# A two-block transformer forward pass on one core: the first weight tile in halves behind four products of zeros, the last three tiles of the last gate by halves of the tokens

## The reference

```python
def first_block(x, p, norm_mix_g, w_in, ...):
    h = rmsnorm(x, norm_mix_g[i])
    u = h @ w_in[i]                       # start of the program
    ...

def second_block(x, p, ln1, w_in, ..., ln3, w_pp, w_pg, rel_bias, ln_f):
    ...
        h3 = rmsnorm_2(x, ln3[i])
        x = x + jax.nn.sigmoid(h3 @ w_pg[i]) * (p[i] @ w_pp[i])   # the last gate
    return rmsnorm_2(x, ln_f)

def rmsnorm_2(x, g):
    xf = x.astype(jnp.float32)
    y = xf * lax.rsqrt(jnp.mean(xf * xf, axis=-1, keepdims=True) + EPS)
    return (y * g.astype(jnp.float32)).astype(x.dtype)
```

## Time and profile before

| | |
|---|---|
| median of 3 runs | 2126.29 us (2119.96 to 2127.86) |
| profiled execution | 2122.81 us, of which the span of the trace is 2120.9 us |
| mean granted TensorE clock | 0.981 of full speed |
| busy share: TensorE, VectorE, ScalarE, GpSimd | 96%, 47%, 37%, 14% |
| first real product of TensorE | 9.12 us after the span's start |
| last product of the last gate | starts at 2095.73 us |

### The profile page before, as it was taken

How to read it: one execution, slowest core, us unless ns; L and a number is a source line. 1 busy time by engine, 2 the same in 40 slices (tenths; PEclk the granted TensorE clock), 3 DMA queues, 4 the chain that set the end, 5 groups by cost and what they waited for, 6 DMA issues and landing times.

```text
span 2120.9 us, 27569 instructions
## 1 busy us (share of the span) xinstructions
PE 2039.4 (96%) x11518; PEld 1625.5 (77%) x11518; DVE 994.1 (47%) x1534; ACT 783.3 (37%) x1233; POOL 293.1 (14%) x292
## 2 busy tenths in 40 slices
PE   7999999999999999999899999998999999999996
PEld 5767677777888778888676788886788888888884
DVE  5665555444643233346845444446643442333354
ACT  5573222113444323235523233335332343322344
POOL 2001221210221001012200000001310220100124
PEclk9999999899999999999999999999999999999998
DMA  4121111112623332223321122221222233222221
GB/s 174 60 70 60 46 52 41 46 42 76 209 87 109 112 102 90 99 100 119 120 67 56 57 70 80 82 88 60 82 97 100 100 120 109 100 90 99 100 80 50
DMA packets 59843, 185.46 MB, mean 87 GB/s; under 512 B 6551, under 2 KB 11799, under 8 KB 59592
## 3 DMA queue, kind: packets, MB, share of 16 engines
q1 hardware_dynamic: 59720, 183.71, 25.5%
HBM read 173.46 MB, written 10.22 MB: 87 GB/s over the span
## 4 chain that ended last, share of the span: by engine, by line
PE 85%; DVE 5%; ACT 4%; issue 3%; POOL 1%; DMA 1%; SPq 0%; DVEq 0%; POOLq 0%; ACTq 0%
PE P L545 24%; PE P L547 23%; PE P L546 23%; DVE AREN L1649 1%; PE P L820 1%; PE P L856 1%; PE P L910 1%; PE P L849 1%; DVE WLO L1656 1%; POOL AREN L2318 1%; PE P L908 1%; PE P L805 1%; ACT WHI L1104 1%; POOL AREN L2321 1%; DVE AREN L1652 1%
## 5 line engine op out<-in xcount | busy, mean ns | idle before, releaser
L545 PE MATMUL P<-HH,WHI 128*128 128x512 f32 x1528 | 628.7, 411 | 22.1 <-DVE WLO L1656 11.8
L547 PE MATMUL P<-HH,WLO 128*128 128x512 f32 x1528 | 602.4, 394 | 0.0
L546 PE MATMUL P<-HL,WHI 128*128 128x512 f32 x1528 | 601.5, 394 | 0.0
L1656 DVE TENSOR_TENSOR WLO<-RAW,WHI 128x1024 fp32r<-128x1024 f32 x303 | 382.3, 1262 | 180.4 <-ACT WHI L1104 178.6
L1104 ACT ACTIVATE WHI<-RAW 128x1024 fp32r<-128x1024 f32 x303 | 318.8, 1053 | 377.3 <-PE P L547 374.3
L545 PEld LDWEIGHTS P<-HH,WHI 128*128 128x128 f32 x1528 | 290.2, 190 | 102.8 <-issue 20.2
L545 PE MATMUL P<-ARR,WHI 128*128 128x512 f32 (+1 forms) x904 | 352.1, 390 | 6.5 <-DVE WLO L1656 2.9
L547 PE MATMUL P<-ARR,WLO 128*128 128x512 f32 (+1 forms) x904 | 350.7, 388 | 0.0
L546 PE MATMUL P<-ARR,WHI 128*128 128x512 f32 (+1 forms) x904 | 350.7, 388 | 0.0
L547 PEld LDWEIGHTS P<-HH,WLO 128*128 128x128 f32 x1528 | 290.3, 190 | 63.6
L546 PEld LDWEIGHTS P<-HL,WHI 128*128 128x128 f32 x1528 | 290.9, 190 | 54.7 <-issue 1.2
(11 more groups left out here) (297 smaller groups left out, 1559.3 us busy)
## 6 DMA issues: line engine op xcount, KB each, us to landing
RAW<-in_w_in_dram SPq DMA_DIRECT2D x118, 512.0 KB, 3.3
RAW<-in_w_ff_dram SPq DMA_DIRECT2D x64, 512.0 KB, 3.3
RAW<-in_w_ml_dram SPq DMA_DIRECT2D x64, 512.0 KB, 3.2
RAW<-in_w_out_dram SPq DMA_DIRECT2D x16, 512.0 KB, 3.4
RAW<-in_w_pg_dram SPq DMA_DIRECT2D x16, 512.0 KB, 3.2
AREN<-in_xT_dram SPq DMA_DIRECT2D x16, 256.0 KB, 6.4
s_gates<-AREN SPq DMA_DIRECT2D x16, 256.0 KB, 2.0
RAW<-in_w_ab_dram SPq DMA_DIRECT2D x8, 512.0 KB, 3.5
```

The costliest lines, as they stand in the source:

```text
L545: e.matmul(out, hi, H[0][:, s], start=first, stop=False)
L546: e.matmul(out, hi, H[1][:, s], start=False, stop=False)
L547: return e.matmul(out, lo, H[0][:, s], start=False, stop=last)
L1656: e.tensor_tensor(WLO[n % NSPL][:, :], RAW[n % NRAW][:, :], WHI[n % NSPL][:, :].bitcast(F32), ALU.subtract).then_inc(*D.dve.sig("wlo", n))
```

## The change

At the start, SyncE loads the first half of tile 0 (slices 0 to 3) ahead of everything, then `x0`, `vec`, `x1`, tile 1, `x2`, `x3`, the second half of tile 0, `x4` to `x7` and tile 2. ScalarE and VectorE split the halves separately. TensorE first multiplies a block of zeros, which GpSimd writes, four times into an unused bank. The second tile runs three rows behind the first instead of two. The sum of squares of the first norm is formed by two engines: GpSimd adds squares 0 to 3, VectorE squares 4 to 7 and the two halves. The squares have eight buffers of their own, and `WHI` of tile 2 stands between squares 3 and 4. The work on `lam` moves behind the first finished tile, and the first norm's total goes to bank 2 instead of 7.

At the end, tiles 5, 6 and 7 of the last gate are multiplied for tokens 0 to 255 first and then for tokens 256 to 511, in six half tiles. The multiplication by the embedding moves from GpSimd to VectorE for these, the last square too. The total of half 0 stands in TensorE's program behind the first half tile of half 1. The outputs are multiplied in five wide operations (one of them, four blocks, on GpSimd), with five stores.

```diff
+def last_rows():
+    yield from lead2(5, 0)
+    for u in range(6):
+        for k in range(8):
+            yield 5 + u, k
+
+def last_steps(j, k):
+    at = {(0, 7): "evac", (1, 0): "sigmoid", (1, 1): "mult", (1, 2): "add", (1, 3): "square", (1, 4): "sum"}
+    return [(5 + u % 3, u // 3, at[j - 5 - u, k]) for u in range(6) if (j - 5 - u, k) in at]
...
-                g = units(("attn",), T_AT, lead2(12, 2), H1, hx("HX"), ev("attn"), (0, 1, 6, 7))
-                for j, k in lead2(12, 2):
+                w.wait_ge(K.pool.at("zero"))
+                for _ in range(4):
+                    e.matmul(bank(3), ar(52)[:, 0:128], ar(52), start=True, stop=True)
+                g = units(("attn",), T_AT, lead2(12, 3), H1, hx("HX"), ev("attn"), (0, 1, 6, 7))
+                for j, k in lead2(12, 3):
                     if (j, k) == (3, 0):
-                        total("n1")
+                        total("n1", 2)
...
+                for half, banks in ((0, (4, 5, 6)), (1, (1, 2, 3))):
                     cs = slice(256 * half, 256 * half + 256)
...
+                    for t, b in zip((5, 6, 7), banks):
+                        w.wait_ge(D.dve.at("wlo", T_PG2 + t), free.get(b))
+                        for k in range(8):
+                            d = row(bank(b)[:, 0:256], T_PG2 + t, k, (H3[k][0][:, cs], H3[k][1][:, cs]), k == 0, k == 7)
+                            if k == 7:
+                                d.then_inc(*D.pe.sig("pg2", t, half))
+                                if half and t == 5:
+                                    last_total(0, 7)
+                            yield
+                last_total(1, 0)
+
+            def last_total(half, b):
...
+                w.wait_ge(N.pool.at("add", "n8", 6, half), K.pool.at("one"), free.get(b))
+                e.matmul(bank(b)[:, 0:256], cst("ones"), ar(acc)[:, cs], start=True, stop=False)
+                w.wait_ge(N.dve.at("sq", "n8", 7, half))
+                e.matmul(bank(b)[:, 0:256], cst("ones"), ar(tmps[1])[:, cs], start=False,
+                         stop=True).then_inc(*N.pe.sig("sum", "n8", half))
...
+            def result(half, i, n):
+                cs = slice(256 * half, 256 * half + 256)
+                y = v3(ar(8, 8), 8)[:, i:n, cs]
+                w.wait_ge(N.act.at("rs", "n8", half), D.act.at("xg", n - 1, half) if n > 5 else D.act.at("xg", n - 1))
+                mul(y, y, ar(6)[:, cs].unsqueeze(1).to_broadcast([128, n - i, 256])).then_inc(*D.dve.sig("y", half, n))
...
+                    if (j, k) == (9, 1):
+                        y = v3(ar(8, 8), 8)[:, 0:4, 0:256]
+                        w.wait_ge(N.act.at("rs", "n8", 0), *[D.act.at("xg", i) for i in range(4)])
+                        mul(y, y, ar(6)[:, 0:256].unsqueeze(1).to_broadcast([128, 4, 256])).then_inc(*D.pool.sig("y"))
...
             def begin():
+                name, i = TILES[0]
+                load("first", 0, RAW[0][:, 0:512], A[name][i, :, 0:512])
                 for j in range(8):
                     load(f"x{j}", 0, ar(j), A["xT"][:, T * j:T * (j + 1)])
                     if j == 0:
                         load("vec", 0, VEC[:, :], A["vecs"])
-                    if j in (0, 3, 7):
-                        weights((0, 3, 7).index(j))
+                    if j == 1:
+                        weights(1)
+                    if j == 3:
+                        load("raw0", 0, RAW[0][:, 512:1024], A[name][i, :, 512:1024])
+                weights(2)
```

More of the change, by code:

```diff
@@ L1264, in dense @@
                 yield from mlp("m", T_ML2, "n6", "H3b", "ln3", "n7")
-                for j, k in [*lead2(7, 0), *[(7, k) for k in range(16)]]:
-                    if j < 7:
+                for j, k in last_rows():
+                    if j < 6:
                         ahead(T_PG2, j, k, True)
@@ L1303, in whi_mg2, with last_rs @@
+            def last_rs(half, b):
+                rs = ar(6)[:, 256 * half:256 * half + 256]
+                w.wait_ge(N.pe.at("sum", "n8", half))
+                e.activation(rs, bank(b)[:, 0:256], ACT.Ln, scale=1.0 / 1024, bias=EPS6).then_inc(
+                    *N.act.sig("ln", "n8", half))
+                w.wait_ge(N.act.at("ln", "n8", half))
+                e.activation(rs, rs, ACT.Exp, scale=-0.5).then_inc(*N.act.sig("rs", "n8", half))
             def whi_mg2(i, k):
@@ L2330, in begin @@
             def begin():
+                e.memset(ar(52), 0.0).then_inc(*K.pool.sig("zero"))
                 for i, (a, v) in enumerate(((EPS6, 1e-6), (EPS5, 1e-5), (EPSG, 64e-5))):
```

215 lines of the change are left out of this document (124 added, 91 removed).

## The result

| | before | after |
|---|---|---|
| median, us (runs) | 2125.97 (8) | 2110.36 (8) |
| lowest to highest | 2119.96 to 2127.86 | 2103.59 to 2119.75 |
| ratio, 95% interval | | 0.9945, 0.9927 to 0.9963 |
| profiled execution, us | 2122.81 | 2113.17 |
| its span, us; mean granted clock | 2120.9; 0.981 | 2111.4; 0.984 |

By the ratio the change made the kernel faster by 0.55% (0.37 to 0.73), which is just past what I had called the limit of no change. (The ratios in this document are the recorded ones and need not be the quotient of the medians, here 0.9927, or of the means, here 0.9936.) The forecast was 2116.5 with a range from 2109 to 2123. The profiled executions differ by 9.6 us, the medians by 15.6. The last sections come back to that difference.

The account below looks back on a forecast made before the run. TensorE, busy in 96% of the span, was taken as the bound, leaving its waits, slow stretches and tail to save. Start 3.0 plus end 5.0 gave 8.0 us: 2114.8 or 2118.3 by baseline, middle 2116.5, range 2109 to 2123.

Parts of the forecast that it names:

- one fall behind it at 1.4: Start: TensorE's clock falls once at the wait before the third row, costing 1.7 us less 0.3 hidden, so 1.4.
- Both old waits: Start: TensorE's waits of 2.22 us for tile 2's `WLO` and 0.87 us for the first norm's root go, gaining 3.1.
- The first term, 1.3: Start: as an unbroken run at 2.4 GHz it begins at 10.6 instead of 11.87, gaining 1.3 us (0.2 to 2.3).
- Steps of 0.43 us after 14 us: Start: listed sign of a wrong prediction, TensorE's products still at the 1.2 GHz pace after 14 us.
- Rival 2: Start: the zeros don't raise the clock; the start brings 1.8, the sum 6.8 us, giving 2118; chance 0.10.
- the loop of half 0: End: half tiles take 2.15 us each on VectorE and ScalarE; tile 7's x ready at 2096.8, with GpSimd's additions 2097.8.
- TensorE waits until 2098.7: End: done with tile 5 at 2093.9, TensorE waits 4 to 5 us at half 0's total before tile 6's second half.
- A fallen clock costs nearly nothing here: End: TensorE's last half tile has 1 us of slack against ScalarE and VectorE.
- The collision with the wide output: End: GpSimd's wide output falls on VectorE's first multiplication of half 1, delaying it 0.8 us more than without.
- Rival 1: Clock holds before row 2, wide output finds VectorE idle: 11.4 us gained, 2113, 0.53% faster; chance 0.22.
- Rival 3: End: the tail's halves don't pay, both end one after the other; tail 1 to 2 us, sum 4.5, 2120; chance 0.15.
- Rival 4: End: twenty VectorE operations each wait out a GpSimd operation (+1.07); tail 21 us longer, net +13, 2138; chance 0.03.

Follow-up runs that it names:

- the second group: Later runs on one chip, before at median 2122.78 and mean 2122.33 us (11 runs), including the unedited whole change again, ratio 0.9957 (0.9939 to 0.9974).
- the groups: Three sets of follow-up runs, kernels of each on the same chip sharing runs of before; before's means were 2121.57, 2122.33 and 2123.13 us.
- the repetition: The whole change run again without any edit, against before: median 2114.09, mean 2113.27 us, ratio 0.9957.
- The start alone: The kernel before with the change's part on the start only, the old end kept: median 2119.13, mean 2118.23 us, ratio 0.9979.
- the end alone: The kernel before with the change's part on the last gate only, the old start kept: median 2114.59, mean 2115.75 us, ratio 0.9973.
- the filled gap: The whole change plus eight unused products in TensorE's wait ahead of the third row: median 2112.28, mean 2111.92 us, ratio 0.9952 against before.
- the version with the early weights: The whole change with tile 7's weights prepared right behind tile 6's: 2111.20 us, ratio 0.9943 against before, tail 47.0 us.
- the banks: The whole change with the sixth and seventh head-recurrence tiles in other banks: median 2107.67, mean 2107.88 us, ratio 0.9933 against before.

## Why the prediction was right, and where it was off

**The sum held**: 8.0 forecast; 9.1 on the means of the second group, 9.6 between the profiled executions. The chances held less well: I gave 0.61 to a change within 0.5% and 0.36 to a faster kernel. The first comparison has 0.55% (0.37 to 0.73), the second group 0.43% (0.26 to 0.61), so the change lies at that limit.

**The median 2110.36 lies 6 us under the forecast.** About half of that is the structure (1 us more than forecast) and the baseline that I took (the middle between the profile and the median; from the profiled execution alone 2114.8, where 2113.17 came). The rest is spread between runs, and that the median lies in the range owes something to its width: the eight runs of before averaged 2125.3 where the groups have 2121.6 to 2123.1, those of after 2111.6 where the repetition has 2113.3. Over the runs of one kernel the time falls by 1.1 to 2.0 us for each 0.001 of the mean granted clock; the eight runs of after had 0.9852, the six of its repetition 0.9845, before in the groups 0.982. At equal clock, 0.985 (a line through each kernel's runs), before stands at 2117.5 to 2118.5 and the whole change at 2112.0 to 2112.6. That comparison takes too much away. The mean counts the tail too, where TensorE idles at the lower level: 20.5 us of it in the trace of before, 9.2 and 8.0 in the two of the whole change. These 11 to 12.5 us are 0.0027 to 0.003 of the mean, about the whole difference between 0.982 and 0.985. The start alone, with the old tail, has 0.9817, and the end alone 0.9852. So the higher mean clock is mostly a mark of the shorter tail, not a second cause beside it.

**The start: 3.0 forecast, 3.1 by the rows.** The terms: landing of tile 1 at 9.0 (8.77); third row not before 12.0 (11.80); wait before it 2.5 to 3.1 (2.27 in after, behind one of 0.35; 2.87 in the repetition); one fall behind it at 1.4 (about 1.6 by the filled gap). Both old waits went, with nothing late in their place. The first term, 1.3, rests on a miscount: the trace of before has 12 products between 9.12 and 14.82, not 13. With 12 the old start is 14.82 - 12 x 0.227 = 12.1 and the new one 11.80 - 1.36 = 10.4, which is 1.7; with the 3.1 of the waits and 1.6 for the fall the sum is 3.2, as measured. "Steps of 0.43 us after 14 us" stood among my signs of being wrong, and they came (13.74 to 16.30); they are the fall that the sum has, so the sign contradicted the forecast. "They cost nothing" held for the zeros; that they bring something did not: they raise the clock and the wait lets it fall, and without them the means are the same (8.7 against 9.1). Rival 2 is refuted as worded, since they do raise it.

**The end: 5.0 forecast, 6.2 and 5.5 by the rows.** The wait before tile 7 was right (2.8 with the 0.55 before tile 6, 3.1 forecast) and so was its being beside the path. The mis-sized term is the loop of half 0: "x of tile 7 is ready at about 2096.8, with GpSimd's additions in the way 2097.8". In before's time it was ready at 2096.9 (VectorE's addition of 2093.09 ends at 2093.51 in after, and the tail began 3.35 earlier). So the half tiles of 2.15 us were right (2.08) and the collision was not: GpSimd's half additions (0.74) overlapped VectorE's operations by less than 0.1 us and lengthened none of them (each took 0.42 to 0.43). That gave 0.9 us. The second half, its total and its root took another 0.9 less than forecast: the first output of half 1 began at 2105.26 + 3.35 = 2108.6, 1.8 before the 2110.4. From it to the end 6.1 us passed and not 5.5, which leaves 1.2: the 6.2 in place of 5.0.

"TensorE waits until 2098.7", 4 to 5 us, was wrong: the first product of the total needs only the sum up to tile 6, which was there sooner. In the repetition it waited 1.96 and 0.58; in after 0.46 and 0.58, since there the clock had fallen behind the wait for `WLO` and TensorE was done with tile 5 later. In the version with the early weights it did wait 4.06. "A fallen clock costs nearly nothing here" holds for a fall among the half tiles; in front of the total it costs the 0.7 us between 46.5 and 47.2.

The collision with the wide output came as forecast: 0.99 us against 0.42, 0.57 more (0.8 forecast). Had VectorE waited until GpSimd's operation ended (2095.76 + 2.40 = 2098.16) and then taken its 0.42, it would have ended at 2098.58; had the two gone at half speed each, at 2098.2. It ended at 2098.44, nearer to waiting. The 1.76 us row did the same: waiting out GpSimd's operation gives 2078.72 + 0.69 = 2079.41, half speed 2078.80, and it ended at 2079.26. The Trainium skill, "SBUF — State Buffer", in its part on who interferes with whom, has the two engines exclude each other for whole instructions; these two rows agree within 0.15 us.

**Rival 1** had no fall and no collision; one fall and one collision came. **Rival 3** is refuted by the end alone (5.8 us on the means, 5.5 by the rows). **Rival 4** likewise: two of the twenty operations were delayed, the one above by 0.57 us and the multiplication of 2088.21 (0.69 us) by 0.27, beside GpSimd's addition for tile 4.

What stays open: why the clock falls in the middle at 318 and 380 us without a long wait ahead, and which falls come in which execution. No run here steers them.

## What to carry to other kernels

Cut a trace at rows that every version has, and compare the pieces: here pieces settled effects of 1 us, where whole runs scatter by 3, and they showed that the lead of one version lay before the edit it seemed to come from. A mean clock counts idle stretches too, so it is no measure of luck between programs that idle differently. A head start in front of a wait only lengthens the wait; find first what the third or fourth step waits for. In a tail, take apart computing and leaving: work cut in halves pays because the first half's output leaves under the second's work, and an edit that brings the last result sooner but bunches the outputs gives it back.

## What was not expected of the hardware

- The time of identical code differs by some 11 us with TensorE's granted clock: the middle took 2031.1 us with 58.0 us at 1.2 GHz, 2026.4 with 44.4, and 2019.7 with 27.3 (the last with the 0.9 of the banks added back). That is 0.35 to 0.4 us for each microsecond at the lower level, less than the half that TensorE alone would lose; that VectorE and ScalarE pace the rest is shown for the head-recurrence tiles only. Traces of the same code lie up to 1.2 us off such a line (2030.1 to 2032.2 us at 58.0).
- Waits of like length end differently: behind 2.22 us in before the clock held, behind 2.85 and 2.90 us at the same place it fell, and behind 2.27 us in after it fell; with products in the gap it held. Behind the wait for `WLO` of tile 7, 2.21 and 2.22 us, it fell in after and held in the repetition.
- VectorE and GpSimd slow each other in wide operations on SBUF: GpSimd's 128x1024 took 2.40 us beside one short VectorE operation and 3.38 beside long ones, and VectorE's four took 5.70 where the same columns without GpSimd take about 3.6 (2.43 for 2048, by the row of after, and half as much for 1024).
- The output transfers ran at 334 to 343 GB/s with all DMA engines busy, so a last megabyte that is ready only at the end costs 3 us (an estimate: 1.05 MB at 340 GB/s).
